# State-space turns: the table of rotations built from 32 steps and doubled twice, in place of products for all 128

## The chip, the cores and the metric

One core of a Trainium2 chip runs the whole program: TensorE (PE), VectorE (DVE), ScalarE (ACT), GpSimd (POOL) and SyncE (SP), which issues most DMAs. The metric is the device time of one launch in microseconds, as the median of several runs. Everything is float32; matmuls take operands split into a high and a low part.

## The reference, cut to what matters

The program is two transformer-like blocks over 1024 positions of width 1024. The change is inside the first block's state-space mixer (`s5_mixer`): a complex linear recurrence h[t] = lam_bar * h[t-1] + b_bar u[t], for 24 groups of 16 channels with 64 complex states each, forward and backward.

```
lam = lax.complex(lam_re.astype(f32), lam_im.astype(f32))
lam_bar = jnp.exp(lam * dt)
...
for d, rev in ((0, False), (1, True)):
    ...
    _, h_dir = lax.associative_scan(_scan_combine, (a, bu), reverse=rev, axis=1)
    states.append(h_dir)
h = states[0] + states[1]
y = (jnp.einsum('bsgp,gcp->bsgc', h.real, c_re.astype(f32))
     - jnp.einsum('bsgp,gcp->bsgc', h.imag, c_im.astype(f32)))
```

## The kernel before

The 1024 positions are cut in 128 chunks (`NCH`) of 8 (`CH`). Within a chunk matmuls do the work. From chunk to chunk the recurrence has a real factor and a rotation by an angle theta that is constant for a state; the kernel multiplies by the rotations, runs a real scan over the 128 chunks on VectorE, and multiplies by the rotations again. The table of rotations `cs` holds for each of 8 rows (4 groups in 2 directions, `GB`) and each chunk j the cosine (`cs[:, 0]`) and the sine (`cs[:, 1]`) of (j + 1) theta.

The 24 groups go in six turns (`TURNS`) of four. Each turn i is, on the engines:

- **VectorE** (`ssm_dve`): `ssm_oo(i+1)`, output weights; `ssm_g(i+1)`, input weights `gs_`, whose adds (L2396, L2397) also need what ScalarE wrote; `ssm_scan(i)`: the product of PSUM with `cs` (L2432), eight scans, and two products that give `av`; then `ssm_cs(i+1)`, the next table. The table is a product of a coarse table `turn_a` (16 entries, rotations by 0, 8, 16 ... chunks) and a fine one `turn_b` (8 entries), each complex, so four real products of 8 x 128 columns (L2417, L2421) and two adds (L2423, L2424). There is one `cs`, so it can be rewritten only after `av` is done. `rotations_dve` makes `turn_a` and `turn_b` once, much earlier, by doubling.
- **TensorE** (`ssm_pe`): `kernel_(i+1)`, small products that need `oo`; `states(i+1)`, 16 transposes of `gs_` into PSUM (L2514) that need VectorE's product of turn i to have freed it, and 32 matmuls (L2519) on ScalarE's copies `gT`; `output(i)` (L2530, L2534), which needs `av`; then `ada_late_pe`, matmuls for the modulation (L486) that belong to another part of the block.
- **ScalarE** (`ssm_act`): `kernel_(i+1)` and `states(i+1)`, copies out of PSUM (`ksb` L2580, `gT` L2586); `g_scaled_act(i+2)`, 64 small copies that scale rows of `bb` into `gs_` (L2406), possible once `gs_` has been transposed; `output(i)`, the gelu into `yg` (L2592).
- **SP and POOL** move `ksb`, `yg` and the `w_ada` tiles by DMA.

Every engine runs its list in the order in which it is written; semaphores tie the lists together (`ss_x` counts ScalarE's scalings, `ss_g` the adds into `gs_`, `ss_y` the outputs, `own` VectorE's own writes before its next read). After the last output and its `ada` matmuls SP starts the loads of the attention.

Of the kernel before, what the change touches and what calls it, by code (L numbers as in the profile page):

```python
# [20 lines left out]
P = 128  # L21
# [10 lines left out]
CH = 8  # L32
# [81 lines left out]
def build(nc, t, out, last=6):  # L114

    ctx = ExitStack()
    with ctx:
# [2207 lines left out]
        def rotations_dve(e):  # L2325

            ta = own(e)
            e.wait_ge(S("pw_ev"), 2)
            of = lambda q: stn[:, q, :].rearrange("p (d i g) -> p i d g", d=2, g=GSUB)
            to = lambda k: turn_b[:, k, :, 0].rearrange("p (i d g) -> p i d g", d=2, g=GSUB)  # L2330
            ta.add(e.tensor_copy(to(0), of(C8)))
            ta.add(e.tensor_copy(to(1)[:, :, 0], of(S8)[:, :, 0]))
            ta.add(e.tensor_scalar(to(1)[:, :, 1], of(S8)[:, :, 1], -1.0, None, ALU.mult))
            ta.add(e.memset(turn_a[:, 0, :, 0], 1.0))
            ta.add(e.memset(turn_a[:, 1, :, 0], 0.0))

            def times(t_, k, lo, n, hi):

                ta.settle()
                x, y = t_[:, :, :, hi:hi + n], turn_y[:, :, :, 0:n]  # L2340
                c, s = (t_[:, j, :, k:k + 1].unsqueeze(1).to_broadcast([P, 2, 2 * G, n]) for j in range(2))
                ta.add(e.tensor_tensor(x, t_[:, :, :, lo:lo + n], c, ALU.mult))
                ta.add(e.tensor_tensor(y, t_[:, ::-1, :, lo:lo + n], s, ALU.mult))
                ta.settle()
                ta.add(e.tensor_tensor(x[:, 0], x[:, 0], y[:, 0], ALU.subtract))
                ta.add(e.tensor_tensor(x[:, 1], x[:, 1], y[:, 1], ALU.add))

            for w in (1, 2, 4):
                times(turn_b, w - 1, 0, w, w)
            ta.settle()  # L2350
            ta.add(e.tensor_copy(turn_a[:, :, :, 1], turn_b[:, :, :, 7]))
            for w in (1, 2, 4, 8):
                times(turn_a, w, 1, min(w, 15 - w), w + 1)
            ta.settle()

        def powers(q, n, d, i):
            return st4(q, n, d, i * GSUB).rearrange("p t g -> p g t").unsqueeze(3).to_broadcast([P, GSUB, n, GC])
# [20 lines left out]
        def ssm_g(e, ta, i):  # L2378

            g0 = i * GSUB  # L2380
            wait(e, S("ss_gp"), 2 * i)
            for d in range(2):
                qr, qi = (PRD + 1, PID + 1) if d == 0 else (PR, PI)
                b = [bb[:, k].rearrange("p (d g) c -> p d g c", d=2)[:, d, g0:g0 + GSUB].unsqueeze(2).to_broadcast([P, GSUB, CH, GC])
                     for k in range(2)]
                x = [gs_[:, k, d].rearrange("p g (t c) -> p g t c", c=GC) for k in range(2)]
                if i == 0:
                    for k in range(2):
                        ta.add(e.tensor_tensor(x[k], powers(qr, CH, d, i), b[k], ALU.mult))
                e.wait_ge(S("ss_g") if d else S("ss_oo"), 4 * i + (2 if d else 4))  # L2390
                for k in range(2):
                    ta.add(e.tensor_tensor(gy[:, k], powers(qi, CH, d, i), b[1 - k], ALU.mult))
                ta.settle()
                if i:
                    e.wait_ge(S("ss_x"), i)
                e.tensor_tensor(x[0], x[0], gy[:, 0], ALU.add).then_inc(S("ss_g"), 1)  # L2396
                e.tensor_tensor(x[1], gy[:, 1], x[1], ALU.subtract).then_inc(S("ss_g"), 1)  # L2397

        def g_scaled_act(e, i):

            for d in range(2):
                q = PRD + 1 if d == 0 else PR
                for g in range(GSUB):
                    r = d * G + i * GSUB + g
                    for k in range(CH):
                        op = e.activation(gs_[:, :, d, g, k * GC:(k + 1) * GC], bb[:, :, r, :], ACT.Copy, scale=stn[:, q + k, r:r + 1])  # L2406
            op.then_inc(S("ss_x"), 1)

        def ssm_cs(e, ta, i):

            us = slice(i * GB, i * GB + GB)
            y = tY[:].rearrange("p k u (a b) -> p k u a b", b=8)
            x = cs[:].rearrange("p k u (a b) -> p k u a b", b=8)
            c, s = (turn_a[:, k, us].unsqueeze(3).to_broadcast([P, GB, 16, 8]) for k in range(2))
            b = [turn_b[:, k, us].unsqueeze(2).to_broadcast([P, GB, 16, 8]) for k in range(2)]
# [7 lines left out]
            ta.add(e.tensor_tensor(cs[:, 0], cs[:, 0], tY[:, 0], ALU.subtract))  # L2423
            ta.add(e.tensor_tensor(cs[:, 1], cs[:, 1], tY[:, 1], ALU.add))  # L2424
            ta.settle()

        def ssm_scan(e, ta, i):

# [64 lines left out]
        def ssm_pe(e):  # L2493
# [81 lines left out]
        def ssm_act(e):  # L2575
# [742 lines left out]
```

## Time and profile before

| | us |
|---|---|
| median of 3 runs | 3294.29 (3293.06 to 3295.58) |
| the profiled execution, its own time | 3297.56 |
| its span | 3295.5 |
| TensorE busy | 3126.9 (95%) |
| VectorE busy | 2179.2 (66%) |
| ScalarE busy | 1400.0 (42%) |
| GpSimd busy | 1695.1 (51%) |

The profile gives one execution on the core. Times are counted from the span's start. The state-space turns lie between about 214 and 395 us of the span; in a timeline row the first number is the start, the second how long the row lasts, and square brackets give the idle time of the engine before it and what ended it. A row that ends in x8 stands for eight instructions in a row.

### The profile page before, as it was taken

How to read it: one execution, taken by the hardware profiler on the slowest of the kernel's cores; microseconds unless marked ns; L12 is line 12 of the kernel's file. 1: busy time of each engine (PE TensorE's matmuls, PEld its weight loads, DVE VectorE, ACT ScalarE, POOL GpSimd, SP SyncE). 2: the span in 40 equal slices, each digit the busy share in tenths (PEclk: the TensorE clock that was granted, in tenths of full speed). 3: DMA queues.
4: the chain of work that ended last, by engine and by line, in shares of the span. 5: the costliest groups of instructions: out<-in, count | busy, mean ns of one | idle time of the engine just before them, and what ended most of it. 6: DMA issues, size and time to landing. Idle time of an engine off the chain costs nothing.

```text
span 3295.5 us, 41468 instructions
## 1 busy us (share of the span) xinstructions
PE 3126.9 (95%) x15015; PEld 2565.2 (78%) x15015; DVE 2179.2 (66%) x2990; ACT 1400.0 (42%) x2651; POOL 1695.1 (51%) x1248
## 2 busy tenths in 40 slices
PE   7978899999999999999999999989999999999998
PEld 4865577778887888788887878878887788887776
DVE  6879772699998133866668871157736866677854
ACT  4136372555443122433434551057723434334642
POOL 3331046766556766754545552344357645445663
PEclk9979899999999999999999999999999999999999
DMA  5534524332233543233336344546442343355433
GB/s 201 125 105 143 134 65 173 130 95 84 90 115 107 210 150 115 84 122 109 103 118 224 110 143 144 171 128 155 112 166 77 103 135 111 96 172 173 155 130 121
DMA packets 338053, 428.47 MB, mean 130 GB/s; under 512 B 62167, under 2 KB 234394, under 8 KB 337092
## 3 DMA queue, kind: packets, MB, share of 16 engines
q1 hardware_dynamic: 261368, 259.81, 27.2%
q10 hardware_dynamic: 71532, 148.90, 12.2%
q0 software_dynamic: 4960, 17.22, 1.6%
q8 instruction: 116, 1.90, 0.2%
q14 instruction: 77, 0.63, 0.1%
HBM read 321.12 MB, written 111.05 MB: 131 GB/s over the span
## 4 chain that ended last, share of the span: by engine, by line
PE 75%; DVE 11%; issue 4%; POOL 3%; ACT 3%; DMA 2%; SPq 1%; ACTq 0%; POOLq 0%; DVEq 0%
PE PS L960 67%; PE PS L2865 3%; PE PS L2882 1%; PE PS L2849 1%; DVE pt L816 1%; PE PS L887 1%; DVE px L824 1%; POOL w_lo L297 1%; POOL dg_ab L3040 1%; DVE dwl L1870 0%; DMA w_raw<-w_out 0%; DVE ss L1310 0%; PE PS L486 0%; ACT gs__360 L2406 0%; POOL x_raw L1236 0%
## 5 line engine op out<-in xcount | busy, mean ns | idle before, releaser
L1331 POOL TENSOR_TENSOR sl<-ss,sh 128x512 fp32r<-128x512 f32 x300 | 452.1, 1514 | 512.9 <-ACT sh L1322 512.9
L297 POOL TENSOR_TENSOR w_lo<-w_raw,w_hi 128x512 fp32r<-128x512 f32 (+1 forms) x284 | 404.3, 1454 | 9.4
L1614 DVE TENSOR_TENSOR cset<-cset,PS 128x512 f32<-128x512 f32 x354 | 231.9, 683 | 254.5 <-PE PS L960 254.3
L293 POOL CAST w_hi<-w_raw 128x2048 fp32r<-128x2048 f32 x71 | 142.5, 2007 | 453.1 <-DMA w_raw<-w_in 161.9
L960 PE MATMUL PS<-h_hi,sh 128*128 128x512 f32 x960 | 373.7, 389 | 0.6 <-issue 0.3
L960 PE MATMUL PS<-h_lo,sh 128*128 128x512 f32 x960 | 373.5, 389 | 0.0
L960 PE MATMUL PS<-h_hi,sl 128*128 128x512 f32 x960 | 373.5, 389 | 0.0
L1836 POOL TENSOR_TENSOR dal<-dar,dah 128x512 fp32r<-128x512 f32 x154 | 237.5, 1551 | 188.0 <-ACT dah L1830 185.5
L1322 ACT ACTIVATE sh<-ss 128x512 fp32r<-128x512 f32 x300 | 189.0, 631 | 338.2 <-DVE ss L1310 327.5
L1310 DVE TENSOR_TENSOR ss<-sr 128x512 f32<-128x512 f32 x300 | 313.7, 1046 | 1.5 <-PE PS L960 1.5
L960 PE MATMUL PS<-x_hi,sh 128*128 128x512 f32 x720 | 281.6, 391 | 14.7 <-DVE x_lo L1302 7.2
L960 PE MATMUL PS<-x_lo,sh 128*128 128x512 f32 x720 | 280.9, 390 | 0.0
L960 PE MATMUL PS<-x_hi,sl 128*128 128x512 f32 x720 | 280.8, 390 | 0.0
L960 PE MATMUL PS<-dwh,dah 128*128 128x512 f32 x616 | 243.0, 394 | 10.7 <-DVE dwl L1870 5.9
L960 PE MATMUL PS<-dwh,dal 128*128 128x512 f32 x616 | 240.6, 391 | 0.0
L960 PE MATMUL PS<-dwl,dah 128*128 128x512 f32 x616 | 240.4, 390 | 0.0
L960 PE MATMUL PS<-h_hi,w_hi 128*128 128x512 f32 x562 | 208.5, 405 | 6.2 <-DVE h_lo L954 6.1
L960 PEld LDWEIGHTS PS<-h_hi,sh 128*128 128x128 f32 x960 | 180.2, 188 | 39.1 <-issue 1.1
L960 PEld LDWEIGHTS PS<-h_hi,sl 128*128 128x128 f32 x960 | 180.2, 188 | 37.4
L960 PEld LDWEIGHTS PS<-h_lo,sh 128*128 128x128 f32 x960 | 180.2, 188 | 37.4
L960 PE MATMUL PS<-h_lo,w_hi 128*128 128x512 f32 x562 | 201.3, 392 | 0.0
L960 PE MATMUL PS<-h_hi,w_lo 128*128 128x512 f32 x562 | 201.2, 392 | 0.0
(406 smaller groups left out, 7358.4 us busy)
## 6 DMA issues: line engine op xcount, KB each, us to landing
sr<-ffn_w_gu SPq DMA_DIRECT2D x80, 512.0 KB, 5.1
dar<-sd SPq DMA_DIRECT2D x154, 256.0 KB, 2.7
w_raw<-w_down SPq DMA_DIRECT2D x44, 512.0 KB, 4.4
sd<-st_odd ACTq DMA_DIRECT2D x22, 1024.0 KB, 4.5
xs<-px ACTq DMA_DIRECT2D x40, 512.0 KB, 2.8
sr<-w_up SPq DMA_DIRECT2D x40, 512.0 KB, 5.1
w_raw<-w_out SPq DMA_DIRECT2D x32, 512.0 KB, 4.7
w_raw<-w_in SPq DMA_DIRECT2D x28, 512.0 KB, 5.9
```

The lines of the kernel that those rows point to most:

```text
L293: e.tensor_copy(w_hi[b][:, 0:n], w_raw[b][:, 0:n]).then_inc(S("w_hi"), 1)
L297: op = e.tensor_tensor(w_lo[b][:, s], w_raw[b][:, s], w_hi[b][:, s].bitcast(F32), ALU.subtract)
L816: e.scalar_tensor_tensor(b.tmp[:], src, stat[:, 2, T:T + 1], b.g[:], ALU.mult, ALU.mult)\
L824: e.tensor_tensor(b.x(T), b.x(T), b.tmp[:], ALU.add).then_inc(S("n_x"), 1)
L887: mm = e.transpose(PS[:, norm_bank(n, q), i * P:(i + 1) * P], xrow(n, hf * 4 + i)[:, k * P:(k + 1) * P], ident[:])
L960: mm = e.matmul(o, a[ai], b[bi], start=start and first, stop=stop and end, skip_group_check=shared)
L1310: e.tensor_tensor(s.sum[p][:], s.part(c, k0, n0), s.part(c, k1, n1), op).then_inc(S("s_sum"), 1)
L1322: e.activation(s.hi[p][:], src, ACT.Copy).then_inc(S("s_hi"), 1)
L1331: e.tensor_tensor(s.lo[p][:], src, s.hi[p][:].bitcast(F32), ALU.subtract).then_inc(S("s_op"), 1)
L1614: e.tensor_tensor(out, out, PS[:, b, :], op).then_inc(S("s_ev"), 1)
L1836: e.tensor_tensor(v.a_lo[a_slot(s)][:], v.a_raw[a_slot(s)][:], v.a_hi[a_slot(s)][:].bitcast(F32), ALU.subtract).then_inc(S("s_op"), 1)
L2865: mm = e.matmul(PS[:, TURN_BANK[q % 3], (k - c0) * P:(k - c0 + 1) * P], a.pr[m % 4][:, (k - k0) * P:(k - k0 + 1) * P], a.dg[m % 2][:], sta ...
```

## The change

The table `cs` of a turn is no longer made by products for all 128 chunks. Products make chunks 0 to 31 only (8 x 32 columns in each instruction, in `ssm_cs`). Two doublings make the rest, with n = 32 and n = 64, by the identities cos((n+m)t) = 2 cos(nt) cos(mt) - cos((n-m)t) and sin((n+m)t) = 2 cos(nt) sin(mt) + sin((n-m)t). The scaling by 2 cos(nt) is done by ScalarE, eight copies with a scale from a table for each doubling (`cs_scaled_act`); VectorE then subtracts or adds the first part of the table read backwards, and one small instruction treats the last column (`cs_twice_dve`). The scales 2 cos(32t) and 2 cos(64t) are kept in two entries of `turn_a`, whose last doubling is gone. A semaphore `ss_tab` takes the place of `ss_dd` and counts the table's steps too, and ScalarE's 64 copies into `gs_` are cut in two halves of 32 with the first scaling of the table between them.

```diff
-            for w in (1, 2, 4, 8):
-                times(turn_a, w, 1, min(w, 15 - w), w + 1)
+            for w in (1, 2, 4):
+                times(turn_a, w, 1, w, w + 1)
             ta.settle()
+            ta.then(e.tensor_scalar(turn_a[:, 0, :, 14:16], turn_a[:, 0, :, 4:9:4], 2.0, None, ALU.mult))
...
                 if i:
-                    e.wait_ge(S("ss_x"), i)
+                    e.wait_ge(S("ss_x"), 3 * i - 1)
...
+        def cs_scaled_act(e, i, lv):
+
+            n = 32 << lv
+            e.wait_ge(S("ss_tab"), 5 * i + (3, 6)[lv])
+            for u in range(GB):
+                r = i * GB + u
+                op = e.activation(cs[:, :, u, n:2 * n], cs[:, :, u, 0:n], ACT.Copy, scale=turn_a[:, 0, r, 14 + lv:15 + lv])
             op.then_inc(S("ss_x"), 1)
 
+        def cs_twice_dve(e, ta, i, lv):
+
+            n = 32 << lv
+            e.wait_ge(S("ss_x"), 3 * i + (1 if lv == 0 else 2 if i + 1 == TURNS else 3))
+            for k, op in ((0, ALU.subtract), (1, ALU.add)):
+                ins = e.tensor_tensor(cs[:, k, :, n:2 * n - 1], cs[:, k, :, n:2 * n - 1], cs[:, k, :, 0:n - 1][:, :, ::-1], op)
+                ta.add(ins) if lv else ins.then_inc(S("ss_tab"), 1)
+            ins = e.tensor_scalar(cs[:, 0, :, 2 * n - 1:2 * n], cs[:, 0, :, 2 * n - 1:2 * n], -1.0, None, ALU.add)
...
-            y = tY[:].rearrange("p k u (a b) -> p k u a b", b=8)
-            x = cs[:].rearrange("p k u (a b) -> p k u a b", b=8)
+            y = tY[:, :, :, 0:32].rearrange("p k u (a b) -> p k u a b", b=8)
+            x = cs[:, :, :, 0:32].rearrange("p k u (a b) -> p k u a b", b=8)
...
                 if i + 1 < TURNS:
                     ssm_oo(e, ta, i + 1)
+                cs_twice_dve(e, ta, i, 0)
+                if i + 1 < TURNS:
                     ssm_g(e, ta, i + 1)
+                cs_twice_dve(e, ta, i, 1)
                 ssm_scan(e, ta, i)
...
-            e.wait_ge(S("ss_dd"), 1)
-            g_scaled_act(e, 1)
+            e.wait_ge(S("ss_tab"), 1)
+            cs_scaled_act(e, 0, 0)
+            for d in range(2):
+                g_scaled_act(e, 1, d)
+            cs_scaled_act(e, 0, 1)
             for i in range(TURNS):
                 if i + 1 < TURNS:
                     kernel_(i + 1)
                     states(i + 1)
-                if i + 2 < TURNS:
-                    g_scaled_act(e, i + 2)
+                    if i + 2 < TURNS:
+                        g_scaled_act(e, i + 2, 0)
+                    cs_scaled_act(e, i + 1, 0)
+                    if i + 2 < TURNS:
+                        g_scaled_act(e, i + 2, 1)
                 output(i)
+                if i + 1 < TURNS:
+                    cs_scaled_act(e, i + 1, 1)
```

ScalarE's list in a middle turn, before: the copies out of PSUM, the 64 scalings into `gs_`, the gelu.

```order
L2580 ACTIVATE ksb<-PS 16x4x240 [waits kd,ss_k]
L2586 ACTIVATE gT_370<-PS 128x1024 [waits ss_gp]
L2586 ACTIVATE gT_371<-PS 128x1024 [waits ss_gp]
L2406 ACTIVATE gs__360<-bb,stn 128x2x16 x64
L2592 ACTIVATE yg_379<-PS 128x512 [waits ss_y]
```

The same turn now (L2606, L2612, L2618 are the copies and the gelu, under new line numbers):

```order
L2606 ACTIVATE ksb<-PS 16x4x240 [waits kd,ss_k]
L2612 ACTIVATE gT_370<-PS 128x1024 [waits ss_gp]
L2612 ACTIVATE gT_371<-PS 128x1024 [waits ss_gp]
L2406 ACTIVATE gs__360<-bb,stn 128x2x16 x32
L2416 ACTIVATE cs<-cs,turn_a 128x2x32 [waits ss_tab]
L2416 ACTIVATE cs<-cs,turn_a 128x2x32 x7
L2406 ACTIVATE gs__360<-bb,stn 128x2x16 x32
L2618 ACTIVATE yg_379<-PS 128x512 [waits ss_y]
L2416 ACTIVATE cs<-cs,turn_a 128x2x64 [waits ss_tab]
L2416 ACTIVATE cs<-cs,turn_a 128x2x64 x7
```

The eight scalings for the first doubling stand between the two halves of the 64, ahead of the half for which VectorE's adds wait (`ss_x`); the eight for the second doubling stand behind the gelu.

VectorE's list in the last turn, before, from the table to the product that reads it:

```order
L2417 TENSOR_TENSOR cs<-turn_a,turn_b 128x1024 [waits ss_av]
L2417 TENSOR_TENSOR cs<-turn_a,turn_b 128x1024
L2421 TENSOR_TENSOR tY<-turn_a,turn_b 128x1024 x2
L2423 TENSOR_TENSOR cs<-cs,tY 128x1024 [waits own]
L2424 TENSOR_TENSOR cs<-cs,tY 128x1024
L2432 TENSOR_TENSOR tY<-PS,cs 128x2048 [waits ss_v,ss_g,own]
```

And now (L2424 and L2426 are the doublings, L2455 the product):

```order
L2440 TENSOR_TENSOR cs<-turn_a,turn_b 128x8x32 [waits ss_av]
L2440 TENSOR_TENSOR cs<-turn_a,turn_b 128x8x32
L2444 TENSOR_TENSOR tY<-turn_a,turn_b 128x8x32 x2
L2447 TENSOR_TENSOR cs<-cs,tY 128x8x32 [waits own]
L2447 TENSOR_TENSOR cs<-cs,tY 128x8x32
L2424 TENSOR_TENSOR cs<-cs 128x8x31 [waits ss_x,ss_tab]
L2424 TENSOR_TENSOR cs<-cs 128x8x31
L2426 TENSOR_SCALAR cs<-cs 128x8
L2424 TENSOR_TENSOR cs<-cs 128x8x63 [waits ss_x]
L2424 TENSOR_TENSOR cs<-cs 128x8x63
L2426 TENSOR_SCALAR cs<-cs 128x8
L2455 TENSOR_TENSOR tY<-PS,cs 128x2048 [waits ss_v,ss_g,own]
```

In this turn nothing of VectorE's other work stands between the table's steps; in the turns ahead `ssm_oo` stands before the first doubling and `ssm_g` between the two.

## Rows read from the trace of the kernel before

**Rows 1.** The page, busy time, share of the span and instructions of each engine.

```profile
PE 3126.9 (95%) x15015; PEld 2565.2 (78%) x15015; DVE 2179.2 (66%) x2990; ACT 1400.0 (42%) x2651; POOL 1695.1 (51%) x1248
```

**Rows 2.** The chain that ended last, in order: start us, us, what.

```profile
239.38 2.30 DVE tY L2432
...
357.22 2.30 DVE tY L2432
...
378.03 3.58 issue
```

**Rows 3.** VectorE's timeline over the second turn.

```profile
268.84 2.29 DVE L2432 TENSOR_TENSOR tY<-PS,cs 128x2048 f32<-128x2048 f32 x1
...
277.47 2.36 DVE L2417 TENSOR_TENSOR cs<-turn_a,turn_b 128x1024 f32<-128x1024 f32 x2
...
284.52 1.43 DVE L2369 TENSOR_TENSOR oo<-stn,cc 128x576 f32<-128x576 f32 x2
...
292.13 0.75 DVE L2376 TENSOR_TENSOR oo<-oo,oy 128x576 f32<-128x576 f32 x1
292.99 1.29 DVE L2392 TENSOR_TENSOR gy<-stn,bb 128x512 f32<-128x512 f32 x2
294.32 0.69 DVE L2396 TENSOR_TENSOR gs__360<-gs__360,gy 128x512 f32<-128x512 f32 x1
...
297.58 0.68 DVE L2397 TENSOR_TENSOR gs__360<-gy,gs__360 128x512 f32<-128x512 f32 x1
298.30 2.29 DVE L2432 TENSOR_TENSOR tY<-PS,cs 128x2048 f32<-128x2048 f32 x1
```

**Rows 4.** VectorE's timeline outside the turns: small instructions, the coarse table's last doubling.

```profile
142.92 0.36 DVE L2346 TENSOR_TENSOR turn_a<-turn_a,turn_y 128x192 f32<-128x192 f32 x1
143.32 0.86 DVE L2342 TENSOR_TENSOR turn_a<-turn_a 128x672 f32<-128x672 f32 x1
...
145.95 1.22 DVE L2170 SCALAR_TENSOR_TENSOR zl<-PS,zh 128x1024 fp32r<-128x1024 f32 x1
...
401.11 0.24 DVE L703 TENSOR_TENSOR gain<-mod,vec 128x8 f32<-128x8 f32 x2
```

**Rows 5.** ScalarE's timeline in the turns.

```profile
221.65 13.65 ACT L2406 ACTIVATE gs__360<-bb,stn 128x32 f32<-128x32 f32 x64
...
260.08 1.28 ACT L2592 ACT_TABLE_LOAD   x1
...
275.88 13.64 ACT L2406 ACTIVATE gs__360<-bb,stn 128x32 f32<-128x32 f32 x64
...
371.10 0.60 ACT L2592 ACTIVATE yg<-PS 128x512 f32<-128x512 f32 x1 [7.01 <-PE PS L2534]
```

**Rows 6.** ScalarE's groups by shape: count, busy us, mean ns, idle before.

```profile
L2406 ACT ACTIVATE gs__360<-bb,stn 128x32 f32<-128x32 f32 x320 | 68.2, 308 | 0.0
...
L854 ACT ACTIVATE xn<-px,stat 128x1024 f32<-128x1024 f32 x14 | 15.4, 1137 | 0.0
...
L2928 ACT ACTIVATE ph_ab<-PS 128x256 fp32r<-128x256 f32 x72 | 27.6, 383 | 14.9 <-PE PS L2865 13.3
```

**Rows 7.** VectorE's timeline, an add of the first turn, the product of the last.

```profile
235.40 0.69 DVE L2396 TENSOR_TENSOR gs__360<-gs__360,gy 128x512 f32<-128x512 f32 x1 [0.18 <-ACT gs__360 L2406]
...
372.91 2.29 DVE L2432 TENSOR_TENSOR tY<-PS,cs 128x2048 f32<-128x2048 f32 x1
```

**Rows 8.** TensorE's timeline: transposes, then output groups of the last two turns.

```profile
271.27 3.65 PE L2514 MATMUL PS<-ident,gs__360 128*128 128x128 f32 x16 [3.35 <-DVE tY L2432]
...
366.66 1.06 PE L2534 MATMUL PS<-av,oo 128*128 128x128 f32 x8
...
383.02 1.86 PE L2534 MATMUL PS<-av,oo 128*128 128x128 f32 x8
```

**Rows 9.** Busy time by stretch: PE, PEld, DVE, ACT, POOL, granted clock, DMA share, GB/s.

```profile
297.80:300.70 2.90, 0.48 (x6) 0.16 (x3) 2.83 (x3) 0.96 (x1) 0.00 (x0) 1.00 0.93 245
300.80:303.80 3.00, 3.00 (x16) 3.00 (x17) 2.97 (x7) 1.02 (x1) 0.00 (x0) 0.56 0.15 34
```

More of the change, by code:

```diff
@@ L2394, in ssm_g, with g_scaled_act @@
                 if i:
-                    e.wait_ge(S("ss_x"), i)
+                    e.wait_ge(S("ss_x"), 3 * i - 1)
                 e.tensor_tensor(x[0], x[0], gy[:, 0], ALU.add).then_inc(S("ss_g"), 1)
                 e.tensor_tensor(x[1], gy[:, 1], x[1], ALU.subtract).then_inc(S("ss_g"), 1)
[L2399 to L2406, printed above, removed]
-            op.then_inc(S("ss_x"), 1)
+        def g_scaled_act(e, i, d):
+            q = PRD + 1 if d == 0 else PR
+            for g in range(GSUB):
+                r = d * G + i * GSUB + g
+                for k in range(CH):
+                    op = e.activation(gs_[:, :, d, g, k * GC:(k + 1) * GC], bb[:, :, r, :], ACT.Copy, scale=stn[:, q + k, r:r + 1])
+            if d:
+                op.then_inc(S("ss_x"), 1)
@@ new lines, in cs_scaled_act @@
+        def cs_scaled_act(e, i, lv):
[4 more added lines that the diff above has]
+                op = e.activation(cs[:, :, u, n:2 * n], cs[:, :, u, 0:n], ACT.Copy, scale=turn_a[:, 0, r, 14 + lv:15 + lv])
+            op.then_inc(S("ss_x"), 1)
+        def cs_twice_dve(e, ta, i, lv):
[5 more added lines that the diff above has]
+            ins = e.tensor_scalar(cs[:, 0, :, 2 * n - 1:2 * n], cs[:, 0, :, 2 * n - 1:2 * n], -1.0, None, ALU.add)
+            if lv:
+                ta.then(ins)
+            else:
+                ins.then_inc(S("ss_tab"), 1)
@@ L2409, in ssm_cs @@
         def ssm_cs(e, ta, i):
             us = slice(i * GB, i * GB + GB)
-            y = tY[:].rearrange("p k u (a b) -> p k u a b", b=8)
-            x = cs[:].rearrange("p k u (a b) -> p k u a b", b=8)
-            c, s = (turn_a[:, k, us].unsqueeze(3).to_broadcast([P, GB, 16, 8]) for k in range(2))
-            b = [turn_b[:, k, us].unsqueeze(2).to_broadcast([P, GB, 16, 8]) for k in range(2)]
+            y = tY[:, :, :, 0:32].rearrange("p k u (a b) -> p k u a b", b=8)
+            x = cs[:, :, :, 0:32].rearrange("p k u (a b) -> p k u a b", b=8)
@@ L2416, in ssm_cs @@
+            c, s = (turn_a[:, k, us, 0:4].unsqueeze(3).to_broadcast([P, GB, 4, 8]) for k in range(2))
+            b = [turn_b[:, k, us].unsqueeze(2).to_broadcast([P, GB, 4, 8]) for k in range(2)]
             for k in range(2):
@@ L2422, in ssm_cs @@
             ta.settle()
-            ta.add(e.tensor_tensor(cs[:, 0], cs[:, 0], tY[:, 0], ALU.subtract))
-            ta.add(e.tensor_tensor(cs[:, 1], cs[:, 1], tY[:, 1], ALU.add))
-            ta.settle()
+            for k, op in ((0, ALU.subtract), (1, ALU.add)):
+                e.tensor_tensor(cs[:, k, :, 0:32], cs[:, k, :, 0:32], tY[:, k, :, 0:32], op).then_inc(S("ss_tab"), 1)
+            e.wait_ge(S("ss_tab"), 5 * i + 3)
         def ssm_scan(e, ta, i):
@@ L2454, in ssm_dve @@
             e.tensor_tensor(dd[:], ident[0:GC, 0:GC].unsqueeze(1).to_broadcast([GC, G, GC]),
-                            drow[:].rearrange("p (g c) -> p g c", c=GC), ALU.mult).then_inc(S("ss_dd"), 1)
+                            drow[:].rearrange("p (g c) -> p g c", c=GC), ALU.mult).then_inc(S("ss_tab"), 1)
             for par in range(2):
@@ L2595, in ssm_act @@
             states(0)
-            e.wait_ge(S("ss_dd"), 1)
-            g_scaled_act(e, 1)
+            e.wait_ge(S("ss_tab"), 1)
+            cs_scaled_act(e, 0, 0)
+            for d in range(2):
+                g_scaled_act(e, 1, d)
+            cs_scaled_act(e, 0, 1)
             for i in range(TURNS):
```

## The prediction

> **What bounds the kernel now.** I read the page first, then the chain that ended last in order of time, then the timelines of VectorE, ScalarE and TensorE over the turns. The page says TensorE is busy for 95% of the span [rows 1]; that average hides the stage of the change. There the chain runs over VectorE: from the product of turn 0 at 239.38 us to that of turn 4 at 357.22 us all its long pieces are VectorE's, and TensorE then stands idle for 3.58 us before the last output, which waits for `av` [rows 2]. VectorE's timeline shows why: one turn takes 298.30 - 268.84 = 29.46 us, with its rows one behind the other [rows 3]; 357.22 - 239.38 = 117.84 is four times 29.46. So a microsecond off VectorE's list is one off the end, but only until something else is late in the same turn. The candidate is ScalarE's 64 scalings. In this turn they end at 275.88 + 13.64 = 289.52 [rows 5], and the add that needs them starts at 294.32 [rows 3]: 4.8 us to spare. In turn 0 there is nothing to spare: they end at 235.30 [rows 5], and the add waited 0.18 us for them and started at 235.40, 0.10 us behind [rows 7].
>
> **The work on VectorE.** Instructions in a row overlap by about 0.08 us (the pair of 1024 columns takes 2.36 and not 2 x 1.22), and the rows give 0.36 us for 192 columns, 0.69 for 512 and 1.22 for 1024 [rows 3, 4], so about 1.04 ns a column. The old table costs 284.52 - 277.47 = 7.05 us a turn [rows 3]. Now:
> - The low 32 chunks: six instructions of 256 columns at 0.42 us. Four products are 4 x 0.34 + 0.08 = 1.44, a wait on its own writes 0.03, two adds 0.76, another wait 0.03: 2.26 us.
> - First doubling: two instructions of 248 columns, 0.33 us each to the next one, and a small one of 8 columns. Two of that size take 0.24 together [rows 4], so 0.16 if waited for and 0.10 if not: 0.76 to 0.82, I take 0.8.
> - Second doubling: two of 504 columns, 0.60 each to the next, the small one 0.16 and 0.03: 1.39 us.
>
> Together 4.45, so VectorE has 2.6 us less in a turn; two small waits disappear behind the new instructions (the gap between 292.13 + 0.67 and 292.99, and the one ahead of the product, 0.3 us together). VectorE alone would make a turn in about 26.7 us.
>
> **The work on ScalarE.** The trace has 32 columns at 308 ns and 1024 columns at 1137 ns, both with a scale from a table [rows 6]: 0.836 ns a column. Each of the 64 costs 13.64 / 64 = 0.213 us to the next one, about 0.10 less than its duration [rows 5]. That gives 0.24 us for 64 columns and 0.293 for 128, so 1.92 us for the eight of the first doubling and 2.44 to the end of the eight of the second. The bounds: 0.213, the price of 32 columns, from below; and from above 0.39, what 256 columns out of PSUM cost (383 ns, less the overlap, plus as much again for the scale) [rows 6]. I take the middle values, since they lie between two rows of the same form. A page of the Trainium skill speaks against this kind of split: "VectorE: DVE Perf Modes", section "The TRN2 errata", says that instructions which read SBUF pay a fixed cost each and should have 512 columns or more. By its table (224 cycles plus the columns, at 1.2 GHz) the new ones cost 0.24 and 0.29 us, an estimate that would leave the sum as it is; the 308 ns for 32 columns show the fixed part, and no run here shows the new shapes.
>
> **A middle turn.** From the product, ScalarE's scalings start after 275.88 - 268.84 = 7.04 us; 13.64 for the 64; 1.92 for the eight now between them; 0.10 to VectorE: the first add can start at 22.70. VectorE is there at 25.48 - 7.05 + 2.26 + 0.8 - 0.2 = 21.3 [rows 3]. So it now waits 1.4 us for ScalarE in each turn, with the remaining adds, the second doubling and the product queued behind. From the first add to the product it was 298.30 - 294.32 = 3.98; the last add is now followed directly (0.11 less) by 1.39 of doubling: 5.26. The turn is 22.70 + 5.26 = **27.96 us**, bound by ScalarE, 1.50 less than before and not 2.8. Four such turns: -6.0 us. The second set of eight stands behind the gelu, at 22.60 + 0.5 + 2.44 = 25.5, and is needed at 26.6: hidden. In the first of the four the gelu also loads its table, 1.28 us [rows 5], and the set is late by 0.35: +0.35.
>
> **The first turn.** ScalarE's eight stand ahead of 64 scalings that were already late: the add goes from 235.40 to 237.32 (+1.92), VectorE being there at 235.9. Behind it the second doubling adds 1.39 - 0.11. The product of turn 0 comes **3.2 us later**.
>
> **The last turn.** Before, 372.91 - 357.22 = 15.69 us from product to product [rows 2, 7]. Now nothing covers the hand-overs, since `ssm_oo` and `ssm_g` have no turn left. After the product: the table starts at 8.63 [rows 3], low part done at 10.89; ScalarE, idle since 364.1 [rows 5], takes 8 x 0.24 + 0.10 and 0.15 for two hand-overs, 13.06; first doubling 0.82 and a hand-over, 13.93. But the gelu stands ahead on ScalarE and waits for TensorE until 371.10 - 357.22 = 13.88; then 0.5, the eight 2.44, 0.10: 16.9. Second doubling 1.39: 18.3. **+2.6 us.**
>
> **Edits at nothing.** The coarse table's last doubling (four instructions, 143.32 to 145.95) becomes one small one, 2.3 us less [rows 4]; the chain is TensorE's there, so it gains nothing, and costs nothing if that cover is gone. The first low table is made while VectorE waits for the Fourier part. SP, POOL and TensorE keep their lists. TensorE's matmuls of `kernel_` end at 298.28 (0.48 into the stretch from 297.80 [rows 9]), 29.4 after the product, and the transposes would be wanted at 27.96 + 2.43 = 30.4: TensorE is the next to be late, with 1 us left.
>
> **The sum.** 3.2 - 6.0 + 0.35 + 2.6 = +0.2 us at the last product, and the same to the end, since output, `ada` and loads follow one another. The profiled execution took 3297.56, its span 3295.5 and 2.06 around it, 3.3 above the median; a difference of 0.2 to its span is one to the median: 3294.3 + 0.2 = 3294.5 us. About 0.2% (6.6 us) is what a measurement can tell from no change.
>
> **Rival 1: TensorE's clock stays up and ScalarE starts earlier.** The 16 transposes of the second turn take 3.65 us after 3.35 us of idle [rows 8]; in the third turn's the granted clock is 0.56, nearly all of it at the level of 1.2 GHz, and 1.00 (2.4 GHz) before [rows 9]. With turns 1.5 us shorter the gaps shrink to 1.9 and 0.9. If the clock then stays at 2.4 GHz, the transposes take about half as long and the scalings start up to 1.7 us earlier, more than the 1.4 for which VectorE waits; a turn would be 26.7. The Trainium skill, "TensorE: Matmul & The Clock Gate", section "What's actually happening", has activity as what releases the throttle, which fits; but the gap of 2.4 us ahead of the third turn's transposes (298.28 to 300.7) did not keep the clock [rows 9], and no shorter one is there to read. The first of the four follows a longer gap than before and stays slow. Three turns at 1.26 less: -3.8, sum -3.6, 3290.7 us. If all four, and the small instructions cheaper, -7.
>
> **Rival 2, slower: the small scalings are dear.** At 0.39 us instead of 0.24 the eight of the first doubling cost 1.2 more in each of six places on the path, and the last second set 0.8: 8.0 in all, 3302.5 us. It counts as slower from +6.6 - 0.2 = 6.4, at 0.11 us more for each. Against it: both neighbours of the same form lie on one line.
>
> **Rival 3: the doublings are free beyond VectorE's own sum**, because ScalarE is never late: 0 + 1.3 in the first turn, -2.8 x 4, +2.6: -7.3, 3287.0. Against it are the 13.64 us of scalings, which cannot start earlier by themselves.
>
> TensorE's clock in the last output adds to all of them: a group takes 1.86 us instead of 1.06 there after the idle time [rows 8], and the gap becomes 6 us instead of 3.6. Two such groups are 1.6 us either way.
>
> **How the numbers follow.** Forecast 0.55 (same). Rival 1 0.22, nearly all same, 0.03 faster. Rival 3 0.05, faster. Rival 2 0.10, slower. The rest, 0.08, is something downstream: 0.02 faster, 0.05 same, 0.01 slower. Faster 0.10, same 0.79, slower 0.11. The range goes from just beyond rival 1 with the clock term (3290.7 - 1.6 and a cheaper table, 3288) to most of rival 2 (3301.5).
>
> **What would show it.** In the profile after: an idle time of some 1.4 us ahead of the add L2397 in turns 1 to 4, put down to ScalarE's `gs_`; products 28.0 us apart; the first near 242.6; 18.3 us between the last two; L2416 at 335 and 388 ns. Products 26.7 apart with transposes under 3 us are rival 1. Wrong would be a turn over 29.5 or L2416 over 0.45 us.

## The result: the kernel became 0.4% slower

| | before | after |
|---|---|---|
| median, five runs of each side by side | 3293.20 us | 3305.10 us |
| lowest to highest | 3291.70 to 3295.58 | 3303.55 to 3312.34 |
| profiled execution, its span | 3297.56, 3295.5 | 3312.34, 3310.3 |
| VectorE busy in the span | 2179.2 us | 2144.7 us |
| ScalarE busy in the span | 1400.0 us | 1428.0 us |

The ratio of after to before over these runs is 1.0040 (95% interval 1.0028 to 1.0053); the medians are 11.9 us apart, where the prediction had 0.2 and a range up to 3301.5. The last two lines of the table show that the change did what it says. The busy line of the page after, beside [rows 1]:

```profile
PE 3130.0 (95%) x15015; PEld 2568.7 (78%) x15015; DVE 2144.7 (65%) x3023; ACT 1428.0 (43%) x2747; POOL 1692.5 (51%) x1248
```

VectorE has 34.5 us less to do, and everything ends later. So VectorE must stand idle where it did not before. Its waits in the stretch from 190 to 410 us say for what (columns: engine, tile and line, what it waited for: us in total, times, longest):

```profile
DVE oo L2370 <- PE PS L2560: 17.0, 4, 4.3
...
DVE cs L2424 <- ACT cs L2416: 6.3, 2, 4.2
...
DVE gs__360 L2397 <- ACT gs__360 L2406: 1.3, 1, 1.3
```

Before, the first two lines were not there at all. The first is the news: four times over 4 us, the first product of `ssm_oo` waits for **TensorE's output matmuls**. The prediction had a wait of 1.4 us in each of these turns at `gs_`, for ScalarE; that wait occurs once, in the first turn, where the prediction had it too.

VectorE's timeline of the second turn after, to be read against [rows 3] (start us, us, instruction, and in brackets the idle time ahead and who ended it):

```profile
273.40 2.29 DVE L2455 TENSOR_TENSOR tY<-PS,cs 128x2048 f32<-128x2048 f32 x1
...
282.02 0.76 DVE L2440 TENSOR_TENSOR cs<-turn_a,turn_b 128x256 f32<-128x256 f32 x2
282.70 0.76 DVE L2444 TENSOR_TENSOR tY<-turn_a,turn_b 128x256 f32<-128x256 f32 x2
283.49 0.76 DVE L2447 TENSOR_TENSOR cs<-cs,tY 128x256 f32<-128x256 f32 x2
288.48 1.43 DVE L2370 TENSOR_TENSOR oo<-stn,cc 128x576 f32<-128x576 f32 x2 [4.23 <-PE PS L2560]
...
296.76 0.73 DVE L2424 TENSOR_TENSOR cs<-cs 128x248 f32<-128x248 f32 x2
297.41 0.17 DVE L2426 TENSOR_SCALAR cs<-cs 128x8 f32<-128x8 f32 x1
...
302.67 1.27 DVE L2424 TENSOR_TENSOR cs<-cs 128x504 f32<-128x504 f32 x2
304.06 2.29 DVE L2455 TENSOR_TENSOR tY<-PS,cs 128x2048 f32<-128x2048 f32 x1
```

The low table is ready at 273.40 + 10.85, 4.8 us sooner after the product than the full table was (284.52 - 268.84 = 15.68). But `oo` starts at 288.48, 15.08 us after the product. Of 4.8 us saved, 0.6 reach the next instruction. Behind it come the two doublings, which cost 2.1 us and hide two small waits of 0.3: 15.58 us from `oo` to the product instead of 13.78. So the turn grows by 1.80 - 0.60 = 1.20, to 30.66 us.

What VectorE waits for is on TensorE's timeline, here after:

```profile
275.83 3.65 PE L2540 MATMUL PS<-ident,gs__360 128*128 128x128 f32 x16 [4.57 <-DVE tY L2455]
279.27 4.63 PE L2545 MATMUL PS<-uT,gT 128*128 128x128 f32 x32
...
287.32 1.06 PE L2560 MATMUL PS<-av,oo 128*128 128x128 f32 x8
```

and the last output group of the same turn before:

```profile
283.08 1.06 PE L2534 MATMUL PS<-av,oo 128*128 128x128 f32 x8
```

`ssm_oo(i + 2)` begins with a wait on `ss_y`, since `oo` has two buffers and the new one is that which output(i) reads. Transposes, state matmuls and output follow the product in TensorE's list and end at 288.38, 14.98 us after it; VectorE starts 0.10 behind. Before, they ended at 284.14, 15.30 after the product, and VectorE was still at its table until 15.68. The table covered the wait with 0.4 us to spare, so no view of before showed a wait there. In the other three turns of before the output ended 14.08 to 14.87 us after the product, which left 0.8 to 1.6 us; in all four turns of after it ends at 14.93 to 15.02.

**Where the 11.9 us are.** The first `oo` product starts anywhere from 217.7 to 221.8 us in the profiled executions, so I compare distances:

| distance, us | before | after | difference |
|---|---|---|---|
| first `oo` product to first product | 18.01 | 20.97 | +2.96 |
| four turns, product to product | 117.84 | 122.67 | +4.83 |
| last two products | 15.69 | 19.42 | +3.73 |

Together +11.5, and the medians differ by 11.9. (The two profiled spans differ by 14.8; from the last product to the end the profiled executions vary between 2916 and 2926 us: 2922.6 before, 2925.4 after. With one profile of each kernel it stays open how much of that is the kernel's.)

The first turn and the last pair after, VectorE's timeline, beside [rows 7]:

```profile
237.53 0.69 DVE L2397 TENSOR_TENSOR gs__360<-gs__360,gy 128x512 f32<-128x512 f32 x1 [1.34 <-ACT gs__360 L2406]
...
242.78 2.29 DVE L2455 TENSOR_TENSOR tY<-PS,cs 128x2048 f32<-128x2048 f32 x1
...
365.45 2.29 DVE L2455 TENSOR_TENSOR tY<-PS,cs 128x2048 f32<-128x2048 f32 x1
...
378.46 0.75 DVE L2424 TENSOR_TENSOR cs<-cs 128x248 f32<-128x248 f32 x2 [2.15 <-ACT cs L2416]
...
383.48 1.28 DVE L2424 TENSOR_TENSOR cs<-cs 128x504 f32<-128x504 f32 x2 [4.19 <-ACT cs L2416]
...
384.87 2.29 DVE L2455 TENSOR_TENSOR tY<-PS,cs 128x2048 f32<-128x2048 f32 x1
```

and ScalarE's in the last pair, beside [rows 5], then its groups of L2416 by shape (count | busy us, mean ns of one | idle before), beside [rows 6]:

```profile
376.34 2.02 ACT L2416 ACTIVATE cs<-cs,turn_a 128x64 f32<-128x64 f32 x8 [3.74 <-DVE cs L2447]
380.52 0.60 ACT L2618 ACTIVATE yg<-PS 128x512 f32<-128x512 f32 x1 [2.16 <-PE PS L2560]
381.01 2.43 ACT L2416 ACTIVATE cs<-cs,turn_a 128x128 f32<-128x128 f32 x8
```
```profile
L2416 ACT ACTIVATE cs<-cs,turn_a 128x128 f32<-128x128 f32 x48 | 14.6, 389 | 3.5 <-DVE cs L2426 3.5
L2416 ACT ACTIVATE cs<-cs,turn_a 128x64 f32<-128x64 f32 x48 | 12.0, 334 | 3.7 <-DVE cs L2447 3.7
```

The last pair is as the prediction described it: the second set of eight stands behind the gelu, which waits for TensorE. Only its size is off, 19.42 and not 18.3, since the gelu started 15.07 us after the product and not 13.88. It waits for the output, and TensorE was slower up to it. Its transposes start 2.44 us after the product in both kernels; the two stretches of 4 us behind their start, before and then after (us, busy time of PE, PEld, DVE, ACT, POOL, granted clock, DMA share, GB/s):

```profile
359.70:363.70 4.00, 4.00 (x24) 4.00 (x25) 3.93 (x10) 1.66 (x2) 0.00 (x0) 0.64 0.17 41
363.70:367.70 4.00, 4.00 (x38) 4.00 (x38) 3.96 (x4) 0.39 (x1) 0.00 (x0) 1.00 0.23 41
```
```profile
367.90:371.90 4.00, 4.00 (x19) 4.00 (x20) 3.93 (x10) 1.35 (x2) 0.00 (x0) 0.50 0.27 50
371.90:375.90 4.00, 4.00 (x32) 4.00 (x31) 3.93 (x8) 0.70 (x1) 0.00 (x0) 0.82 0.09 15
```

The clock was 0.50 and 0.82 where it had been 0.64 and 1.00. TensorE had idled 4.92 us ahead of them, in a longer turn, and 2.82 before; that the longer idle time did it is not shown. In b_free below, which keeps the lists of before, the idle time there is 3.41 us and the gelu starts 15.10 us after the product, as late as here.

### The profile page after: what moved, and what is told of

It is laid out like the page before. It is cut to its first block, busy times and chain, and to the rows that moved or that the text cites. A ratio compares the mean times of both kernels' runs of the same rounds, so it can differ in the third digit from the quotient of the medians.

```text
span 3310.3 us, 41599 instructions
## 1 busy us (share of the span) xinstructions
PE 3130.0 (95%) x15015; PEld 2568.7 (78%) x15015; DVE 2144.7 (65%) x3023; ACT 1428.0 (43%) x2747; POOL 1692.5 (51%) x1248
## 4 chain that ended last, share of the span: by engine, by line
PE 71%; DVE 7%; issue 4%; POOL 3%; DMA 2%; ACT 2%; SPq 0%; ACTq 0%; POOLq 0%; DVEq 0%
PE PS L960 63%; PE PS L2899 3%; PE PS L2916 1%; PE PS L2883 1%; DVE pt L816 1%; PE PS L887 1%; DVE px L824 1%; POOL w_lo L297 1%; POOL dg_ab L3074 1%; DVE dwl L1870 1%; DMA w_raw<-w_out 0%; DVE ss L1310 0%; PE PS L486 0%; POOL x_raw L1236 0%; DVE pr_ab L3016 0%
## 5 line engine op out<-in xcount | busy, mean ns | idle before, releaser
L1310 DVE TENSOR_TENSOR ss<-sr 128x512 f32<-128x512 f32 x300 | 304.2, 1015 | 1.4 <-PE PS L960 1.4
```

The costliest lines, as they stand in the source:

```text
L1310: e.tensor_tensor(s.sum[p][:], s.part(c, k0, n0), s.part(c, k1, n1), op).then_inc(S("s_sum"), 1)
```

## Experiments

My theory after the result: the wait for `ss_y` is the whole difference between 27.96 and 30.66 us a turn. Rivals: the doublings cost more than their instructions, or ScalarE or TensorE's clock sets the turn with or without that wait. All runs are compared with the kernel before on the same chip. The four turns are the distances between the first five products, the last pair is the distance between the last two, and +10.89 means 10.89 us after the product of the turn.

### Without the wait: a_free, and the same in the kernel before: b_free

```
-            wait(e, S("ss_y"), i - 1)
+            wait(e, S("ss_k"), i - 1)
...
-                            mm = e.matmul(o, oo[i % 2][:, h, d, g, m0:m0 + CH, :].rearrange("p t c -> p (t c)"), av[:, h, d, g, :],
+                            mm = e.matmul(o, uT[:, g0 + g, :], av[:, h, d, g, :],
```

> The changed kernel, with one dependence taken away: the output matmuls of a turn take as weights the inputs uT instead of oo (so the output of the mixer is another one), and ssm_oo then waits for kernel_ alone, not for the output two turns back. Theory (the shorter table uncovered the wait of ssm_oo for TensorE's output, 4.2 us a turn): the idle time ahead of L2370 is gone, VectorE reaches the first add at about 21.3 us after the product and waits 1.4 us for ScalarE there, products are 28.0 us apart, the last product comes near 374.5 us and the time is 3295 us. Rival (VectorE is held by something else at that place, such as av or its own writes, or ScalarE's scalings slow it): products stay 30.6 apart, 3305 us.

> The kernel before with the same dependence taken away (output matmuls read uT in place of oo). Theory: the full table's 7.05 us of products ended just behind TensorE's output, so the wait was covered and nothing is gained: products 29.46 apart, 3293 us. Rival (the outputs' weights or the wait cost something of their own): the same gain of 2 us or more a turn as in the changed kernel, 3283 us.

Measured: a_free's turns are 28.26, 27.85, 27.69 and 27.95 us, the last pair 17.79; 3296.09 us, ratio 1.001 (1.000 to 1.002). VectorE's timeline of its second turn:

```profile
268.00 2.29 DVE L2455 TENSOR_TENSOR tY<-PS,cs 128x2048 f32<-128x2048 f32 x1
...
278.89 1.43 DVE L2370 TENSOR_TENSOR oo<-stn,cc 128x576 f32<-128x576 f32 x2
...
290.59 0.69 DVE L2397 TENSOR_TENSOR gs__360<-gs__360,gy 128x512 f32<-128x512 f32 x1 [1.42 <-ACT gs__360 L2406]
```

`oo` follows the low table at +10.89, and now the forecast wait is there, 1.42 us for ScalarE. These are the distances that I had predicted: turns near 27.96, the last pair 17.8 for 18.3. b_free's turns are 29.47, 29.45, 29.47 and 29.46, ratio 1.0001 (0.9992 to 1.0011): in the kernel before the wait cost nothing. So the change itself laid it bare. One thing stays open: by its distances a_free should lie 0.9 us below before (21.13 + 111.75 + 17.79 against 151.54), and its median is 4.3 above, with an interval from 0 to 6.6 us for the ratio. Between the profiled executions of a_free and b_free the stretch from the last product to the end differs by 3.6 us (2925.6 and 2922.0); 0.9 of it is there when the last output ends (15.89 and 15.03 us after the product), the rest lies in code that neither run edits.

### Only the low 32 chunks, no doubling: a_low

```
             ssm_g(e, ta, 0)
+            ta.then(e.memset(cs[:], 1.0))
             ssm_cs(e, ta, 0)
...
-                cs_twice_dve(e, ta, i, 0)
...
-                cs_twice_dve(e, ta, i, 1)
...
-                    cs_scaled_act(e, i + 1, 0)
...
-                    cs_scaled_act(e, i + 1, 1)
```

> The changed kernel without any doubling: only the low 32 chunks of the table are made, and the rest keeps the ones it was filled with once ahead of the turns (so the mixer's result is another one). It measures what the shorter products alone can give. Theory: ssm_oo still waits for TensorE's output until 15.1 us after the product, so 4.8 us less of VectorE work give only 0.7 us a turn and 0.1 at small gaps: products 28.6 apart, the last pair 10.9, 3285 us. Rival (the sum of the prediction, VectorE's own work decides): products 24.7 apart, 3269 us.

Measured: turns 27.82, 29.20, 27.94 and 27.96; 3284.06 us, ratio 0.9977 (0.9967 to 0.9986). Even with no doubling anywhere, `oo` starts only 14.05 to 15.43 us after the product; in the second turn:

```profile
269.12 2.29 DVE L2455 TENSOR_TENSOR tY<-PS,cs 128x2048 f32<-128x2048 f32 x1
...
284.55 1.43 DVE L2370 TENSOR_TENSOR oo<-stn,cc 128x576 f32<-128x576 f32 x2 [4.58 <-PE PS L2559]
```

A turn is the end of the output plus 13.8 us, and VectorE's saving ahead of `oo` is worth only what lies between its old start and that end. The rival, that work removed from VectorE counts in full (turns of 24.7), falls.

### ScalarE's part: a_half

```
+        def g_half_act(e, i):
+            r = G + i * GSUB
+            e.activation(gs_[:, :, 1, 0, 0:GC], bb[:, :, r, :], ACT.Copy, scale=stn[:, PR, r:r + 1]).then_inc(S("ss_x"), 1)
...
-                        g_scaled_act(e, i + 2, 1)
+                        g_half_act(e, i + 2)
```

This is on top of a_free.

> The kernel with the freed oo (output matmuls read uT), and ScalarE leaves out 31 of the 32 scalings of the second direction from turn 2 on (so these input weights are others). Theory (with the wait gone ScalarE's 64 and 8 scalings hold the turn at 27.9): VectorE then never waits for ScalarE, products are 26.4 to 26.9 apart (VectorE's own work 26.4, or TensorE's transposes, which must follow the modulation matmuls and kernel_), 5 us below the freed kernel, 3290 us. Rival (VectorE's own work is the 27.9): 27.9 apart, 3295 us.

Measured: four turns of 26.48, 26.49, 26.48 and 26.48 with no wait of VectorE in them; 3287.80 us, ratio 0.9984 (0.9974 to 0.9993). That is VectorE's own sum; the prediction had put it at about 26.7. So behind the wait for the output there is a second limit, ScalarE at 27.9, and a third, VectorE at 26.5.

### The output earlier on TensorE: a_out1st, a_fill, a_fill1

The output's inputs are ready when the scans end, well ahead of the state matmuls that stand before it in TensorE's list. a_out1st puts it between transposes and state matmuls:

```
-                    states(i + 1)
+                    turned(i + 1)
                 output(i)
+                if i + 1 < TURNS:
+                    states(i + 1)
```

> The changed kernel with TensorE's list in another order: output(i) stands between the transposes of turn i + 1 and its 32 state matmuls, instead of behind them; nothing else changes. Theory: the output starts when av is done (8.7 us after the product) and ends at 13.2, so ssm_oo starts at 13.2 and not 15.1; products 28.8 us apart, the last pair about 18 apart; last product near 376, 3296.5 us. Rival (the order on TensorE doesn't matter, ScalarE or VectorE hold the turn at 30.6): 3305 us, or more since the state matmuls end later.

Measured: turns 30.76, 31.24, 30.71 and 30.72, no gain at all; 3304.54 us, ratio 1.0044 (1.0029 to 1.0058). TensorE's timeline in the second turn (product at 270.20), and the busy time of PE, PEld, DVE, ACT, POOL with the granted clock, DMA share and GB/s of two stretches:

```profile
278.89 0.77 PE L2558 MATMUL PS<-uT,mm 128*128 128x128 f32 x2 [4.32 <-issue]
279.45 1.92 PE L2562 MATMUL PS<-av,oo 128*128 128x128 f32 x8
```
```profile
274.60:278.80 4.20, 0.00 (x0) 0.00 (x0) 4.16 (x8) 4.20 (x18) 0.00 (x0) 0.74 0.15 32
278.90:283.20 4.30, 4.30 (x20) 4.30 (x21) 2.12 (x6) 4.30 (x21) 0.00 (x0) 0.50 0.28 55
```

The output did start earlier, 8.69 us after the product. But TensorE had stood idle for 4.32 us until `av` was there, the granted clock in the stretch behind is 0.50 (1.2 GHz), its first two groups take 1.92 us instead of 1.06, and all of it ends at +15.56, where it ended at +14.98 in the changed kernel. In the other three turns it ends at +15.03 to +15.07, against +14.93 to +15.02. The theory was now that the state matmuls ahead of it had kept the clock up.

So the two next kernels put independent matmuls into that gap, the modulation's tiles that otherwise follow the output: two in a_fill, one in a_fill1 (the cut below is a_fill1's; a_fill has `q0 + 2`).

```
+                q0 = ADA[i - 1] if i else 0
+                if i + 1 < TURNS:
+                    ada_late_pe(e, q0, q0 + 1)
+                    q0 += 1
                 output(i)
```

> The kernel with output(i) ahead of the state matmuls again, and now two of the turn's modulation tiles (8 matmuls, 3.4 us) fill TensorE's gap between the transposes and the output, in which it stood idle for 4.32 us. Theory (in that run the output came early, 8.7 us after the product, but ran at a granted clock of 0.5 after the idle time and so ended no earlier): the clock stays up, the output takes 4.6 us and not 6.7, ssm_oo starts 13.4 us after the product, products 28.9 apart, last pair 18, 3297 us. Rival (it is the place of the output and not the clock): 30.7 apart, 3304 us.

> The kernel with output(i) ahead of the state matmuls and one modulation tile (4 matmuls) between the transposes and the output, where two tiles ended only 10.0 us after the product, 1.4 after av was there. Theory (the output's end is set by its start and by the granted clock): one tile ends at about 8.5, the output starts at 8.8 with the clock at 1.0 and ends at 13.4, products are 28.9 apart, the last pair about 18; 3297 us against 3293 of before. Rival (ssm_oo can't start before 15 for another reason): 30.6 apart, 3304 us.

Measured, a_fill: turns 30.20, 30.46, 30.59 and 30.66; 3306.88 us, ratio 1.0041 (1.0027 to 1.0055), a miss. a_fill1: 29.14, 29.36, 29.10 and 29.16; 3302.02 us, ratio 1.0027 (1.0016 to 1.0037). The second turn of a_fill on TensorE (product at 270.89), and one stretch:

```profile
276.91 2.37 PE L486 MATMUL PS<-adl,cz 128*8 128x512 f32 x4
279.12 1.88 PE L486 MATMUL PS<-act,cz 128*8 128x512 f32 x4
280.93 0.49 PE L2558 MATMUL PS<-uT,mm 128*128 128x128 f32 x2
```
```profile
279.00:283.00 4.00, 4.00 (x23) 2.35 (x22) 2.68 (x7) 4.00 (x20) 1.06 (x2) 1.00 0.51 137
```

and of a_fill1 (product at 268.94):

```profile
274.95 3.00 PE L486 MATMUL PS<-adl,cz 128*8 128x512 f32 x4
277.89 0.49 PE L2558 MATMUL PS<-uT,mm 128*128 128x128 f32 x2
...
281.56 1.06 PE L2562 MATMUL PS<-av,oo 128*128 128x128 f32 x8
```

The clock is 1.00 in both (in a_fill1 from 277.90 to 282.60). So a_fill's turns come out at its rival's number for another reason: with two tiles the output starts only at +10.0 and `oo` at +14.9. With one it starts at +8.95 and `oo` at +13.8 in this turn (13.5 to 13.8 in the four), and the turns are the expected 28.9 to within 0.5. a_fill1's time is still 9.0 us above before, where its distances (21.18 + 116.76 + 17.79) give 4.2: 5 us unexplained, as in a_free.

### The independent half of `ssm_oo` first: a_oy1st

```
-            wait(e, S("ss_y"), i - 1)
...
+                if not d:
+                    wait(e, S("ss_y"), i - 1)
+                for k in range(2):
+                    ta.add(e.tensor_tensor(o[:, k, d], powers(qr, 9, d, i), c[k], ALU.mult))
```

The first pair of `oy` products, which does not touch `oo`, goes ahead of the wait.

> The changed kernel, but ssm_oo makes its first two products oy (L2374) ahead of the wait for TensorE's output, since they don't write the buffer that the output reads. Theory (the turn is held by that wait, with 8.3 us of oo behind it): 1.34 us of work moves into the idle time, which shrinks from 4.2 to 2.9, and products are 29.3 us apart; 5.3 us less in four turns, 3300 us. Rival (something behind oo holds the turn, such as ScalarE's scalings): products stay 30.6 apart, 3305 us.

Measured: turns 28.96, 28.22, 29.36 and 28.39; 3299.27 us, ratio 1.0022 (1.0012 to 1.0031). 7.7 us of the four turns' 122.67 come back. The 1.34 us moved in each turn are 5.4 of them; the rest is TensorE's, whose output ended at +13.80 to +14.95 instead of +14.93 to +15.02.

### The ends: a_ends

```
-            for w in (1, 2, 4):
-                times(turn_a, w, 1, w, w + 1)
+            for w in (1, 2, 4, 8):
+                times(turn_a, w, 1, min(w, 15 - w), w + 1)
...
+            m = 16 if i in (0, TURNS - 1) else 4
...
+                if 0 < i < TURNS - 1:
+                    cs_twice_dve(e, ta, i, 0)
```

The first and the last table are made by products again, as before the change; only the four in the middle are doubled.

> The changed kernel with the tables of the first and the last turn made by products for all 128 chunks as before, and the doublings in turns 1 to 4 alone. It separates the ends from the middle. Theory: the first product comes 3.2 us earlier, the last pair is 15.7 apart instead of 19.4, the turns between stay at 30.7 (29.9 where the first doubled table is read): 7 us off, 3298 us, which leaves 4 x 1.2 = 5 above before. Rival (the ends don't matter, as their waits are covered): 3305 us.

Measured: last pair 15.69 as before, first product 236.48 (b_free 236.39, a_free 239.74); turns 29.94, 30.31, 30.50 and 30.61; 3296.37 us, ratio 1.0012 (1.0002 to 1.0022). The first add on VectorE, beside [rows 7]:

```profile
232.50 0.69 DVE L2397 TENSOR_TENSOR gs__360<-gs__360,gy 128x512 f32<-128x512 f32 x1 [0.17 <-ACT gs__360 L2406]
```

So the two ends of the change cost 3.0 (by the distance above) and 3.7 us, and with both gone the middle turns are still 3.5 us longer than before (121.36 against 117.84); 2.7 us were measured.

### Putting the parts together: a_best1, a_oyends, a_best2

a_oyends is a_ends with a_oy1st; a_best1 adds a_fill1; a_best2 is a_best1 with TensorE's order of the last pair as before:

```
+                if i + 2 < TURNS:
+                    ada_late_pe(e, q0, q0 + 1)
+                    q0 += 1
+                elif i + 1 < TURNS:
+                    states(i + 1)
                 output(i)
```

> All three together: tables of the first and the last turn by products, output ahead of the state matmuls with one modulation tile between, oy ahead of the wait. Theory: the first product as early as in the kernel before, the wait at oo down to some 1 us, turns of 28.0 to 28.3 set by ScalarE, the last pair 15.7 apart: 5 to 6 us below before, 3287.5 us. If the output can't come earlier than 15: middle turns of 28.7 to 29.3, 3290 to 3293 us.

> The changed kernel with the tables of the first and the last turn by products and oy ahead of the wait; TensorE's list as it was. From the runs so far: turns of 28.2 to 29.4 as with oy first alone, last pair 15.7: 4 x 28.8 + 15.7 = 130.9 against 133.5 before, 2.6 us below before, 3291 us. If the two edits undo each other (the clock at the transposes differs), 3293 us or more.

> All three edits together, but in the last pair of turns TensorE's list is as it was (state matmuls ahead of the output), since there the product waited 1.45 us for the state matmuls. Theory: products of turns 0 to 4 28.2, 28.2, 27.8 and 27.8 apart as in the run before, last pair 15.7 instead of 17.1; 127.7 us from the first product to the last against 133.5 before; 5 to 6 us below before, 3288 us. Rival (the ends were set by something else): last pair 17.1, 3290 us.

| | four turns | last pair | median, before | ratio |
|---|---|---|---|---|
| a_best1 | 28.24, 28.19, 27.81, 27.81 | 17.11 | 3290.01, 3293.00 | 0.9990 (0.9981 to 0.9999) |
| a_oyends | 28.60, 29.61, 28.49, 29.57 | 15.69 | 3290.65, 3293.00 | 0.9991 (0.9982 to 1.0000) |
| a_best2 | 28.26, 27.82, 29.27, 27.81 | 15.69 | 3286.61, 3292.39 | 0.9984 (0.9974 to 0.9994) |

a_best2 is the fastest kernel that leaves nothing out, 5.8 us below before by the medians (2 to 9 us by the interval) and some 18 below after. The two edits to the lists, `oy` first and the tile, were not tried in the kernel before; there VectorE has no wait in the turns that they could fill. VectorE in its second turn, and in the third where the gain is missing:

```profile
264.16 2.29 DVE L2459 TENSOR_TENSOR tY<-PS,cs 128x2048 f32<-128x2048 f32 x1
277.60 1.43 DVE L2375 TENSOR_TENSOR oo<-stn,cc 128x576 f32<-128x576 f32 x2 [1.12 <-PE PS L2568]
...
291.98 2.29 DVE L2459 TENSOR_TENSOR tY<-PS,cs 128x2048 f32<-128x2048 f32 x1
306.87 1.43 DVE L2375 TENSOR_TENSOR oo<-stn,cc 128x576 f32<-128x576 f32 x2 [2.57 <-PE PS L2568]
```

and TensorE in the third:

```profile
294.42 1.94 PE L2545 MATMUL PS<-ident,gs__360 128*128 128x128 f32 x16 [1.99 <-DVE tY L2459]
296.28 1.88 PE L486 MATMUL PS<-adl,cz 128*8 128x512 f32 x4
300.68 0.77 PE L2564 MATMUL PS<-uT,mm 128*128 128x128 f32 x2 [2.51 <-issue]
```

After an idle time of 1.99 us the transposes ran at 2.4 GHz, so transposes and tile were done early, TensorE stood idle for 2.51 us ahead of the output, and the output began at half the clock (0.50 from 300.60 to 302.80): 29.27 us for the turn instead of 27.8. But the third turn of a_best1 has the same lists and the same times up to there, 1.98 us of idle time, 1.94 us for the transposes, 2.51 us of idle time ahead of the output; its clock stayed at 1.00, its output ended at +13.41, and the turn took 27.81. So the idle time alone does not decide whether the clock falls, and the order of these lists leaves the turn open to it.

## Why the prediction was wrong

**The step that failed is "A middle turn", in its clause "VectorE is there at 25.48 - 7.05 + 2.26 + 0.8 - 0.2 = 21.3".** It subtracts the old table and adds the new pieces as if nothing stood between table and add but VectorE's own list. `ssm_oo`, which stands in between, begins with a wait for TensorE. The code of before has that line, and the trace has both ends of it, TensorE's at +15.30 and VectorE's at +15.68; I read neither of them, since no view listed a wait. With them the same working gives the right answer: `oo` 0.1 us behind the end of the output and 13.78 + 1.80 behind that, 31.0 us a turn from this turn's +15.30 and 29.8 from the earliest of the four, +14.08. Both are slower than the 29.46 of before, against 30.66 measured. "Wrong would be a turn over 29.5" was the mark that showed it.

Point by point:
- **What bounds the kernel:** right for VectorE as the chain; "The candidate is ScalarE's 64 scalings" named the second limit (27.9 in a_free), not the first.
- **The work on VectorE:** 4.45 us of new work forecast. The low part starts at 282.02 and would be over at 284.25, 2.23 for the 2.26; the doublings together 2.1 us for the 2.2. The sum behind "VectorE alone" is 29.46 - 2.6 - 0.3 = 26.56 and not 26.7; a_half measured 26.48.
- **The work on ScalarE:** 334 and 389 ns against 335 and 388. The Trainium skill ("VectorE: DVE Perf Modes", section "The TRN2 errata") asks for 512 columns or more because of a fixed cost for each instruction. The trace has such a fixed cost, 0.17 us for 8 columns on VectorE, but the smaller instructions cost what the rows of before gave, and it did not decide the result.
- **ScalarE's bound of 27.96:** right, but only once the other wait is away (27.69 to 28.26 in a_free; 26.5 in a_half, with 31 of the 64 scalings gone). The +0.35 for the gelu's table is 0.22 us of waiting in a_free's first turn, and nothing in the changed kernel.
- **First turn:** +3.0 for +3.2.
- **Last turn:** the mechanism right, +3.73 for +2.6. The mis-sized term is the gelu at 13.88, 15.07 in its place: I carried TensorE's time over from one turn of one execution. In b_free, with the lists of before, it is 15.10, so 13.88 was the early end of what that list gives. In a_free, where the transposes took 1.94 us, the pair is 17.79.
- **Edits at nothing, "TensorE is the next to be late, with 1 us left":** it looked at the right engine and at the wrong meeting point. I compared TensorE with the next product, where it had room, and not with `oo`, where it had none.
- **Rival 1:** its mechanism exists, though not in the changed kernel, where the idle times ahead of the transposes grew to 4.3 to 4.9 us in the middle turns. In a_free gaps of 2.4 us and more still lost the clock, one of 1.62 kept it, and the 16 transposes then took 1.94 us instead of 3.65. It brought no shorter turn in a_best1, where turns of 27.81 us have transposes of 1.94 and of 2.46 us.
- **Rival 2:** excluded, both prices as forecast. **Rival 3** (ScalarE never late) falls in a_free.
- **TensorE's clock in the last output:** it was to cost 1.6 us. The idle time grew from 3.58 to 6.12 us, and the output ended 15.13 us after the product where it had ended at 15.03: nothing to speak of.
- **The chance of 0.11 for slower:** too small, since I had given "something downstream" slower 0.01, with no look at the waits between the two ends of the edit.

## What to carry to other kernels

Before work is cut from an engine's list, read every wait that the code places between the cut and the next thing that matters, the ones for a buffer to come free too, and compare both arrival times at each: a wait that is covered, here by 0.4 to 1.6 us, appears in no list of waits, and here it took 4.2 of the 4.8 us that were saved. What is added behind such a wait counts in full, though what is removed ahead of it does not, so moving work across it can be a loss with a smaller sum. Try then to move independent work in front of the wait (the `oy` products, 5.4 us of the 7.7 gained here), and to apply the cheaper form only to the passes in which other work covers its hand-overs (a_ends).

## What the runs showed of the hardware

- A dependent burst on TensorE that is moved ahead into an idle stretch can lose all that it gains: 8.69 instead of 10.34 us after the product at its start, yet 15.56 instead of 14.98 at its end, with the granted clock at 0.50 behind 4.32 us of idle. With the stretch filled the clock was 1.00, but the filler has to be done when the data arrive: with one modulation tile the output ended at +13.41 to +13.68, with two at +14.51 to +14.96.
- The idle time ahead of the 16 transposes does not by itself give their time. Up to 1.11 us (a_half, a_out1st) they took 1.94 us, the time at 2.4 GHz. From 1.40 to 1.99 us they took anything from 1.94 to 3.60 us: 1.98 us of idle gave 1.94 and 2.46 in a_best1 and 3.60 in a_best2. From 2.36 us up they took 2.97 to 3.65 us. What decides between these wasn't tried.
- Times of a kernel can lie some 5 us above the sum of its distances in the stretch it changes (a_free and a_fill1), while in the other kernels the sums hold within 2 or 3 us. Where these 5 us are stays open; the stretch behind the last product varies by up to 9 us between the profiled executions (2916.2 to 2925.6).
